# Experts mixed with tokens on the partitions, the residual carried into the banks by identity products, and the last norm taken per partition

## The chip, the cores and the metric

The kernel runs on one core of one Trainium2 chip. The metric is the device time of one execution in microseconds (us). Engines are named as the profile names them: PE is TensorE (matrix products), PEld its weight loads, DVE is VectorE, ACT is ScalarE, POOL is GpSimd, SP is SyncE, which here only issues transfers. A "bank" is one of the eight accumulators that PE writes, 128 partitions by 512 fp32 columns.

## The reference, cut to what matters

The program is a three-layer model on 256 tokens of width 1024, all in fp32. Only its end is touched. There, each of 16 experts picks its 32 tokens, the weighted expert outputs are added to the residual, and a last RMS norm over the 1024 features of each token ends the program:

```
x = x + expert_choice_ffn(rms_norm(x, norm_ffn), router, exp_gate, exp_up, exp_down)
return rms_norm(x, norm_final)

def rms_norm(x, g, eps=1e-6):
    y = x * rsqrt(mean(x * x, axis=-1) + eps)     # mean over the 1024 features of a token
    return y * g

# in expert_choice_ffn, for expert e with its 32 tokens idx[e] and their weights vals[e]
y[e]  = (silu(xg[e] @ w_gate[e]) * (xg[e] @ w_up[e])) @ w_down[e] * vals[e]
out   = zeros(256, 1024); out[idx[e]] += y[e]      # over all experts
```

## The kernel before, in words

**Layout.** The residual is held transposed, in the tile `residual_T` (`m.xT`): eight pieces of 128 features on the partitions by 256 tokens. `normed_T` (`hT`) has the same shape and holds normed activations or squares. A sum over the features of a token is then a sum over partitions, which PE makes by a product with a matrix of ones (`sum_of_squares`, L461 to L470).

**Weights.** All weights come from memory in 378 chunks of 1 MB (16 tiles of 128x128). 370 of them go through a ring of six slots, `weight_ring`, issued by SP in the loop L2217 to L2224: a slot is filled again once PE has signalled, on its next fed product, that it has used it up (`Feed.pass_on`, L397). The last eight chunks are brought early into a region of the arena by ACT (L1451).

**Experts.** For each expert x (L1100 to L1127), PE makes gate, up and down products, each from four chunks, the 32 tokens of the expert being the stationary side (`quarters`). The four quarters of the output width stand on four groups of 32 partitions. In between come two pairs of transposes (`flip`, L416), whose results ACT and DVE copy. DVE copies the expert's output to `m.ye` (L2110, signal `e_y`). Then eight products "mix" the expert into banks 4 to 7 (L1124 to L1126): the stationary side is a piece of `ye`, the moving side is `m.comb`, the 32 rows by 256 tokens that say which token takes which output with which weight. The banks hold features on the partitions and tokens along the row, and are accumulated over all 16 experts. They were cleared by products with zeros (L1098).

**The end.** After the last mix (signal `e_mix`), DVE adds each bank to the residual (L2115), DVE and ACT square the eight pieces (L2118, L1482), PE sums the squares over the partitions into bank 5 (L1132), ACT takes the root of 128x256 copies of the sums (L1485), DVE its reciprocal (L1555), DVE multiplies the eight pieces by it and by the gain (`normalise`, L1558), PE transposes all of them back to tokens on the partitions (16 flips, L1138), ACT and DVE copy the banks to the arena (L1487, L2123), and SP stores each half of 128 tokens (L2225 to L2229). Each step waits for the one before it on another engine. The engines' orders are written out by hand; nothing else plans them.

Of the kernel before, what the change touches and what calls it, by code (L numbers as in the profile page):

```python
# [9 lines left out]
ALU = mybir.AluOpType  # L10
ACT = mybir.ActivationFunctionType
# [51 lines left out]
def columns():  # L63
# [9 lines left out]
        ("q_norm", 1), ("k_norm", 1), ("norm_ffn_2", KD), ("norm_final", KD), ("rel_bias", HEADS),  # L73
# [79 lines left out]
X_FLIP = {"in": 0, "out": 4}  # L153
# [6 lines left out]
class Signals:  # L160


    def __init__(self, nc, ctx):
        def sem(name):
# [13 lines left out]
        (self.x_flip, self.xT, self.square, self.square_v, self.sumsq, self.both, self.weights, self.root, self.normed, self.h, self.res, self.first_a, self.first_v,  # L178
         self.mod_sum, self.mod_row, self.mod_cols, self.mod, self.mod_acc) = [sem(n) for n in (
            "x_flip", "xT", "square", "square_v", "sumsq", "both", "weights", "root", "normed", "h", "res", "first_a", "first_v",  # L180
# [38 lines left out]
        self.out_even, self.out_odd = [sem(n) for n in ("out_even", "out_odd")]  # L219
# [17 lines left out]
class Memory:  # L237


    def __init__(self, nc, ctx):  # L240
# [91 lines left out]

        a = Arena(area, n)
        self.htok_ = a.take(NT * D)
        self.htok = tiles(self.htok_, D)
# [68 lines left out]
def tensor_program(e, m, s, feed):  # L404
# [193 lines left out]
    e.wait_ge(s.late, 16)  # L598
# [501 lines left out]
    for x in range(EXPERTS):  # L1100
# [23 lines left out]
        for j in range(4):  # L1124
            for a in range(2):
                ins = mm(B[4 + j][:, a * T:(a + 1) * T], m.ye[32 * j:32 * j + 32, a * P:(a + 1) * P], m.comb[32 * j:32 * j + 32, :], False, False)  # L1126
        ins.then_inc(s.e_mix, 1)  # L1127

    e.wait_ge(s.xT, 8 * NORM_OUT + KD)
    for k in range(KD):  # L1132
        if k % 2:
            e.wait_ge(s.square, squares_before(NORM_OUT) + k + 1)
        else:
            e.wait_ge(s.square_v, k // 2 + 1)
        sum_of_squares(NORM_OUT, k)
    for j in range(NT):  # L1138
        for q in range(2):
            for c in range(4):  # L1140
                e.wait_ge(s.normed, 8 * NORM_OUT + 4 * q + c + 1)
                ins = flip(B[2 * j + q][:, c * P:(c + 1) * P], hT[:, 4 * q + c, j * P:(j + 1) * P])
            ins.then_inc(s.x_flip, 1)


def scalar_program(e, m, s, dram):
# [1240 lines left out]
```

## Time and profile before

| what | value |
|---|---|
| median of 3 runs | 1902.39 us (1899.36 to 1904.59) |
| the profiled execution's own time | 1904.66 us |
| its span, first to last instruction | 1902.9 us |
| PE busy | 1573.6 us, 83% of the span |
| DVE busy | 549.2 us, 29% |
| ACT busy | 259.3 us, 14% |
| read from memory | 402.69 MB |
| mean granted TensorE clock | 0.906 of full speed |

The times of the program fall into three stages: up to about 1415 us the layers before the experts, then the 16 experts up to 1882.8 us, and the end behind the last mix, 20.1 us. Which engine or transfer bounds a stage is read from the rows of that stage, not from the shares of the whole span.

### The profile page before, as it was taken

The numbers are of one execution on the slowest core, as the hardware profiler recorded it, in microseconds if no ns is written. First come the engines' busy times: TensorE is split into PE (matmuls) and PEld (weight loads), VectorE is DVE, ScalarE is ACT, GpSimd is POOL, SyncE is SP. The second block draws the span as 40 slices with busy tenths as digits, with TensorE's granted clock in tenths as the row PEclk, the third lists the DMA queues.
The fourth block names the chain that finished last, engine by engine and source line by source line (L and its number), as shares of the span: only waits on it lengthen the run. The fifth ranks groups of instructions, "written<-read, shape, count | busy, mean of one in ns | idle before, by whom it ended". The sixth has DMA issues, their size and how long they took to land.

```text
span 1902.9 us, 25312 instructions
## 1 busy us (share of the span) xinstructions
PE 1573.6 (83%) x11140; PEld 1152.3 (61%) x11140; DVE 549.2 (29%) x1199; ACT 259.3 (14%) x618; POOL 72.0 (4%) x96
## 2 busy tenths in 40 slices
PE   7979999998879999999878879998866656666666
PEld 4857788886637888878656657776732222222223
DVE  3670444301132311033647554323220000000002
ACT  2330100002212000001323222220100000000001
POOL 0120000000000000000110111200000000000000
PEclk8989999998979999999988999999988787778787
DMA  8466578744343644333100001323629999999992
GB/s 359 155 258 248 218 279 318 278 142 155 133 155 121 236 151 155 138 128 133 68 24 24 2 24 45 114 108 126 250 87 421 422 420 421 421 421 420 419 421 105
DMA packets 57485, 405.39 MB, mean 213 GB/s; under 512 B 6168, under 2 KB 8344, under 8 KB 8864
## 3 DMA queue, kind: packets, MB, share of 16 engines
q1 hardware_dynamic: 53984, 390.35, 52.5%
q10 hardware_dynamic: 3392, 13.42, 1.8%
q8 instruction: 88, 1.44, 0.3%
q14 instruction: 21, 0.17, 0.0%
HBM read 402.69 MB, written 1.06 MB: 212 GB/s over the span
## 4 chain that ended last, share of the span: by engine, by line
PE 65%; DMA 23%; DVE 9%; ACT 2%; issue 1%; POOL 0%; ACTq 0%; SPq 0%; POOLq 0%; DVEq 0%
PE bank L409 63%; DMA weight_ring<-weights 22%; DVE arena L1499 3%; PE bank L416 2%; DVE arena L1505 2%; ACT arena L1151 1%; DVE arena L1502 1%; DVE arena L1830 1%; DVE rstd L1555 1%; DVE normed_T L1505 0%; DMA arena<-x 0%; DVE rstd L1897 0%; DVE arena L1692 0%; DVE arena L1828 0%; ACT normed_T L1151 0%
## 5 line engine op out<-in xcount | busy, mean ns | idle before, releaser
L409 PE MATMUL bank<-normed_T,weight_ring 128*128 128x256 f32 x2640 | 608.1, 388 | 27.0 <-ACT arena L1151 12.4
L409 PEld LDWEIGHTS bank<-normed_T,weight_ring 128*128 128x128 f32 x2640 | 504.5, 194 | 108.1 <-ACT arena L1151 18.0
L409 PE MATMUL bank<-weight_ring,arena 128*32 128x256 f32 (+1 forms) x2976 | 270.0, 484 | 146.9 <-DMA weight_ring<-weights 138.5
L409 PE MATMUL bank<-arena,weight_ring 128*128 128x256 f32 x1456 | 329.6, 384 | 9.7 <-ACT arena L1151 6.8
L409 PEld LDWEIGHTS bank<-arena,weight_ring 128*128 128x128 f32 x1456 | 279.5, 193 | 51.0 <-issue 8.5
L409 PEld LDWEIGHTS bank<-weight_ring,arena 128*32 128x32 f32 (+1 forms) x2976 | 100.7, 132 | 302.9 <-DMA weight_ring<-weights 206.5
L1151 ACT ACTIVATE arena<-bank 128x256 f32<-128x256 f32 (+4 forms) x299 | 109.9, 374 | 1171.2 <-PE bank L409 625.1
L409 PE MATMUL bank<-arena 64*64 64x64 f32 (+7 forms) x3096 | 225.7, 283 | 28.4 <-DVE arena L1499 14.1
L409 PEld LDWEIGHTS bank<-arena 64*64 64x64 f32 (+5 forms) x3096 | 167.3, 155 | 97.5 <-issue 48.6
L1505 DVE SCALAR_TENSOR_TENSOR arena<-arena,bank 128x256 f32<-128x256 f32 x141 | 59.4, 422 | 544.1 <-PE bank L409 276.4
L416 PE MATMUL bank<-packed_consts,arena 128*128 128x128 f32 (+1 forms) x166 | 42.8, 358 | 65.1 <-DVE arena L1502 35.6
L416 PEld LDWEIGHTS bank<-packed_consts,arena 128*128 128x128 f32 (+1 forms) x166 | 22.6, 171 | 98.8 <-DVE arena L1502 46.1
L1505 DVE SCALAR_TENSOR_TENSOR residual_T<-bank,modulation,residual_T 128x256 f32<-128x256 f32 x32 | 15.5, 484 | 217.9 <-PE bank L409 217.9
L1505 DVE SCALAR_TENSOR_TENSOR arena<-weight_ring,silu_c,arena 128x1024 f32<-128x1024 f32 x49 | 62.8, 1282 | 1.0
L1151 ACT ACTIVATE normed_T<-residual_T 128x256 f32<-128x256 f32 x52 | 21.2, 415 | 291.3 <-DVE residual_T L1505 277.0
L409 PE MATMUL bank<-weight_ring,silu_c_copies 128*32 128x512 f32 (+1 forms) x256 | 39.7, 712 | 19.9 <-DMA weight_ring<-weights 19.9
L1151 ACT ACTIVATE arena<-arena 128x256 f32<-128x256 f32 (+3 forms) x93 | 42.0, 470 | 54.2 <-DVE arena L1692 32.2
L1499 DVE TENSOR_TENSOR arena<-arena 128x256 f32<-128x256 f32 (+4 forms) x98 | 41.1, 423 | 11.2 <-ACT arena L1151 8.0
L2110 DVE COPY arena<-bank 128x256 f32<-128x256 f32 x16 | 6.8, 425 | 129.1 <-PE bank L409 129.1
L1499 DVE TENSOR_TENSOR arena<-bank,packed_consts 128x256 f32<-128x256 f32 (+1 forms) x85 | 28.4, 369 | 41.8 <-PE bank L409 41.4
L2133 POOL TENSOR_TENSOR arena<-arena,packed_consts 128x512 f32<-128x512 f32 (+1 forms) x28 | 28.8, 1036 | 271.8 <-DVE arena L1499 192.0
L409 PE MATMUL bank<-normed_T,packed_consts 128*128 128x256 f32 x112 | 33.3, 403 | 5.6 <-DVE residual_T L1499 3.1
(119 smaller groups left out, 637.5 us busy)
## 6 DMA issues: line engine op xcount, KB each, us to landing
weight_ring<-weights SPq DMA_DIRECT2D x370, 1024.0 KB, 10.2
arena<-ahead ACTq DMA_DIRECT2D x8, 1024.0 KB, 18.0
packed_consts<-packed ACTq DMA_DIRECT2D x1, 2852.0 KB, 13.6
arena<-bias_by_distance ACTq DMA_DIRECT2D x2, 1024.0 KB, 7.0
arena<-x SPq DMA_DIRECT2D x1, 1024.0 KB, 5.2
out<-arena SPq DMA_DIRECT2D x2, 512.0 KB, 2.6
packed_consts<-packed SPq DMA_DIRECT2D x1, 254.5 KB, 2.8
bias_by_distance<-arena ACTq DMA_DIRECT2D x1, 16.0 KB
```

Source lines behind the costliest of these rows:

```text
L409: return e.matmul(out, lhsT, rhs, start=start, stop=stop, skip_group_check=True)
L416: return e.transpose(out, in_, ident[0:n, 0:n])
L1151: return e.activation(out, in_, f, **kw)
L1499: return e.tensor_tensor(out, a, b, op)
L1502: return e.tensor_scalar(out, a, s1, s2, op0, op1) if s2 is not None else e.tensor_scalar(out, a, s1, None, op0)
L1505: return e.scalar_tensor_tensor(out=out, in0=a, scalar=sc, in1=b, op0=op0, op1=op1)
L1555: link(e.reciprocal(m.rstd[:, :], m.rstd[:, :]))
L1830: link(e.reciprocal(tiles(inv_, P), F))
L2110: e.tensor_copy(m.ye, B[3][:, 0:QW]).then_inc(s.e_y, 1)
L2133: return e.tensor_tensor(out, a, b, op)
```

## The change: what it does

The mix is turned round: `m.comb` (128 of its token columns) is now the stationary side and `m.ye` the moving one, so banks 4 to 7 hold tokens on the partitions and features along the row. Bank 4 + j holds features 256 j to 256 j + 255, for tokens 0 to 127 in its left half and 128 to 255 in its right half.

The residual is brought into the same banks by PE: behind the mix of each of the first four experts stand four products with the identity matrix, 128x128 each, that transpose pieces of `residual_T` and add them to the bank.

The last norm then works per partition. ACT squares each half bank with an accumulator output (eight instructions, one number per token each). DVE multiplies each bank by the final gain, which now comes as a 128x1024 array, the same row on every partition; ACT's queue brings it in (512 KB, behind the gather copy k = 1) to the left half of `normed_T`. DVE adds up the 128x8 sums to 128x2, ACT takes the roots, DVE the reciprocals; then DVE scales tokens 0 to 127 and ACT tokens 128 to 255, each in one instruction of 128x1024, in place in `residual_T`, and SP stores each half from there. The eight columns of `norm_final` leave the packed constants.

```
@@ tensor_program
-                ins = mm(B[4 + j][:, a * T:(a + 1) * T], m.ye[32 * j:32 * j + 32, a * P:(a + 1) * P], m.comb[32 * j:32 * j + 32, :], False, False)
+                ins = mm(B[4 + j][:, a * T:(a + 1) * T], m.comb[32 * j:32 * j + 32, a * P:(a + 1) * P], m.ye[32 * j:32 * j + 32, :], False, False)
         ins.then_inc(s.e_mix, 1)
-    e.wait_ge(s.xT, 8 * NORM_OUT + KD)
-    for k in range(KD):
...
-        sum_of_squares(NORM_OUT, k)
-    for j in range(NT):
-        for q in range(2):
-            for c in range(4):
-                e.wait_ge(s.normed, 8 * NORM_OUT + 4 * q + c + 1)
-                ins = flip(B[2 * j + q][:, c * P:(c + 1) * P], hT[:, 4 * q + c, j * P:(j + 1) * P])
-            ins.then_inc(s.x_flip, 1)
+        if x < 4:
+            for a in range(NT):
+                for i in range(2):
+                    mm(B[4 + x][:, a * T + i * P:a * T + (i + 1) * P], m.xT[:, 2 * x + i, a * P:(a + 1) * P], ident, False, False)
@@ scalar_program
         act(m.xall[:, k * 512:(k + 1) * 512], B[k % 4][:, :], ACT.Copy).then_inc(s.x_odd, 1)
+        if k == 1:
+            e.dma_start(m.final_gain, dram["final_gain"]).then_inc(s.late, 16)
...
     e.preload_act_table(ACT.Sqrt)
-    for k in range(1, KD, 2):
-        e.wait_ge(s.xT, 8 * NORM_OUT + k + 1)
-        act(hT[:, k, :], xT[:, k, :], ACT.Square).then_inc(s.square, 2)
-    root(NORM_OUT)
-    res = m.htok
-    for j in range(NT):
-        e.wait_ge(s.x_flip, X_FLIP["out"] + 2 * j + 1)
-        act(res[:, j, 0:512], B[2 * j][:, :], ACT.Copy).then_inc(s.out_even, 1)
+    sums, roots = m.y_stat[:, 0:4 * NT], m.y_stat[:, 4 * NT:5 * NT]
+    e.wait_ge(s.e_mix, EXPERTS)
+    for j in range(4):
+        if j >= 2:
+            e.wait_ge(s.y_gain, 4 - j)
+        for a in range(NT):
+            act(m.y_sq[:, 4 * a + j, :], B[4 + j][:, a * T:(a + 1) * T], ACT.Square, accum_out=sums[:, 4 * a + j:4 * a + j + 1]).then_inc(s.square, 1)
+    e.wait_ge(s.sumsq, NORM_OUT)
+    act(roots, roots, ACT.Sqrt, scale=1.0 / D, bias=m.col("eps")).then_inc(s.root, 1)
+    e.wait_ge(s.normed, 8 * NORM_OUT + 1)
+    act(m.yg[:, D:2 * D], m.yg[:, D:2 * D], ACT.Copy, scale=roots[:, 1:2]).then_inc(s.out_row[1], 1)
@@ vector_program
+    def with_gain(j):
+        yg = m.yg.rearrange("p (m j n) -> p m j n", m=NT, j=4)[:, :, j, :]
+        return tt(yg, tiles(B[4 + j][:, :], T), m.final_gain[:, j * T:(j + 1) * T].unsqueeze(1).to_broadcast([P, NT, T]), ALU.mult)
+
+    e.wait_ge(s.late, LATE["final_gain"])
     e.wait_ge(s.e_mix, EXPERTS)
-    for j in range(4):
-        o = m.xT_[:, 2 * j * T:(2 * j + 2) * T]
-        tt(o, B[4 + j][:, :], o, ALU.add).then_inc(s.xT, 2)
-    for k in range(0, KD, 2):
-        e.wait_ge(s.xT, 8 * NORM_OUT + k + 2)
-        tt(hT[:, k, :], xT[:, k, :], xT[:, k, :], ALU.mult).then_inc(s.square_v, 1)
-    inverse_root(NORM_OUT)
-    normalise(hT, col("norm_final", 0, KD), s.normed)
-    for j in range(NT):
-        e.wait_ge(s.x_flip, X_FLIP["out"] + 2 * j + 2)
-        e.tensor_copy(m.htok[:, j, 512:1024], B[2 * j + 1][:, :]).then_inc(s.out_odd, 1)
+    with_gain(3).then_inc(s.y_gain, 1)
+    with_gain(2).then_inc(s.y_gain, 1)
+    for j in range(2):
+        e.wait_ge(s.square, squares_before(NORM_OUT) + NT * (j + 1))
+        with_gain(j).then_inc(s.y_gain, 1)
+    sums, roots = m.y_stat[:, 0:4 * NT], m.y_stat[:, 4 * NT:5 * NT]
+    e.wait_ge(s.square, squares_before(NORM_OUT) + 4 * NT)
+    e.tensor_reduce(roots, tiles(sums, 4), AX, ALU.add).then_inc(s.sumsq, 1)
+    e.wait_ge(s.root, NORM_OUT + 1)
+    e.reciprocal(roots, roots).then_inc(s.normed, 1)
+    e.wait_ge(s.normed, 8 * NORM_OUT + 1)
+    e.wait_ge(s.y_gain, 4)
+    ts(m.yg[:, 0:D], m.yg[:, 0:D], roots[:, 0:1], None, ALU.mult).then_inc(s.out_row[0], 1)
@@ sync_program
-        e.wait_ge(s.out_even, j + 1)
-        e.wait_ge(s.out_odd, j + 1)
-        e.dma_start(dram["out"][0, j * P:(j + 1) * P, :], m.htok[:, j, :]).then_inc(s.stored, 16)
+        e.wait_ge(s.out_row[j], 1)
+        e.dma_start(dram["out"][0, j * P:(j + 1) * P, :], m.yg[:, j * D:(j + 1) * D]).then_inc(s.stored, 16)
@@ Memory
+        a = Arena(self.hT_, KD * T)
+        self.final_gain, self.y_stat = a.take(D), a.take(5 * NT)
+        self.yg = self.xT_
```

Where the instructions stand now. First PE's queue around the mix of expert 0 (each row a run of like instructions; "arena x8" is the mix, `packed_consts` holds the identity). Before:

```order
L409 MATMUL bank<-weight_ring,arena 32x256 x32
L409 MATMUL bank<-arena 128x256 x8
L409 MATMUL bank<-weight_ring,arena 32x256 x32
L416 MATMUL bank<-packed_consts,arena 128x128 x2
L409 MATMUL bank<-weight_ring,arena 32x256 x32
```

After:

```order
L415 MATMUL bank<-weight_ring,arena 32x256 x32
L415 MATMUL bank<-arena 128x256 x8
L415 MATMUL bank<-packed_consts,residual_T 128x128 x4
L415 MATMUL bank<-weight_ring,arena 32x256 x32
L422 MATMUL bank<-packed_consts,arena 128x128 x2
L415 MATMUL bank<-weight_ring,arena 32x256 x32
```

Four products stand between the mix of expert 0 and the gate products of expert 1, and the same behind experts 1 to 3. Next DVE's queue behind the copy of the last expert's output (the first row of each piece). Before:

```order
L2110 COPY arena<-bank 128x256
L1499 TENSOR_TENSOR residual_T<-bank,residual_T 128x512 x4
L1499 TENSOR_TENSOR normed_T<-residual_T 128x256 x4
L1555 RECIPROCAL rstd<-rstd 128x256
L1505 SCALAR_TENSOR_TENSOR normed_T<-residual_T,packed_consts,rstd 128x256 x8
L2125 COPY arena<-bank 128x512 x2
```

After:

```order
L2109 COPY arena<-bank 128x256
L1498 TENSOR_TENSOR residual_T<-bank,normed_T 128x2x256 x4
L2126 TENSOR_REDUCE normed_T<-normed_T 128x2
L2128 RECIPROCAL normed_T<-normed_T 128x2
L1501 TENSOR_SCALAR residual_T<-residual_T,normed_T 128x1024
```

The 256-wide reciprocal, the eight 256-wide products and the two copies are gone; a reduction and a reciprocal of two columns and one product of 1024 columns stand in their place. PE's queue ends with the last mix. ACT's queue from the last expert on, before:

```order
L1151 ACTIVATE arena<-bank 128x256 x32
L1481 ACT_TABLE_LOAD
L1151 ACTIVATE normed_T<-residual_T 128x256 x4
L1151 ACTIVATE rstd<-bank,packed_consts 128x256
L1151 ACTIVATE arena<-bank 128x512 x2
```

After:

```order
L1145 ACTIVATE arena<-bank 128x256 x32
L1477 ACT_TABLE_LOAD
L1145 ACTIVATE arena,normed_T<-bank 128x256 x8
L1145 ACTIVATE normed_T<-normed_T,packed_consts 128x2
L1145 ACTIVATE residual_T<-residual_T,normed_T 128x1024
```

ACT now squares all eight pieces, straight from the banks, and scales one half of the result.

## Rows read from the trace of the kernel before

**Rows 1.** Busy time by stretch: us, then each engine's, PEclk, DMA share, GB/s.

```profile
1500.00:1860.00 360.00, 228.45 (x2520) 89.95 (x2512) 22.84 (x69) 7.90 (x24) 0.00 (x0) 0.79 1.01 421
1868.60:1882.80 14.20, 12.53 (x164) 6.09 (x164) 1.70 (x4) 1.94 (x3) 0.00 (x0) 0.83 0.00 1
1882.80:1902.90 20.10, 10.34 (x32) 7.20 (x32) 10.22 (x19) 3.33 (x7) 0.00 (x0) 0.69 0.13 52
1396.00:1415.00 19.00, 17.99 (x39) 7.40 (x37) 3.04 (x6) 2.39 (x4) 0.20 (x1) 0.92 0.00 0
```

**Rows 2.** Chain of waits behind the last mix: start us, us, what.

```profile
1881.58 1.24 PE bank L409 x16
...
1882.92 2.50 DVE residual_T L1499 x4
...
1885.84 5.39 PE bank L409 x16
...
1891.76 1.76 DVE rstd L1555
...
1894.09 4.97 PE bank L416 x16
...
1899.08 0.69 DVE arena L2125
```

**Rows 3.** Timeline of SP's issues at the end; then DMAs by kind, us to landing.

```profile
1898.16 2.03 SPq L2228 DMA_DIRECT2D out<-arena  x2
...
out<-arena SPq DMA_DIRECT2D x2, 512.0 KB, 2.6
```

**Rows 4.** Timeline of ACT in a softmax: start us, us, what.

```profile
1250.05 0.48 ACT L1151 ACTIVATE arena<-bank,arena 128x256 f32<-128x256 f32 x1 [1.29 <-DVE arena L2006]
1250.42 0.19 ACT L1151 ACTIVATION_READ_ACCUMULATOR arena<-bank,arena 128x1 f32 x1
1250.52 0.46 ACT L1151 ACTIVATE arena<-bank,packed_consts 128x256 f32<-128x256 f32 x1
```

**Rows 5.** ACT's instructions by form: busy us, mean ns, idle before.

```profile
L1151 ACT ACTIVATE arena<-bank 128x256 f32<-128x256 f32 x235 | 88.1, 383 | 1076.6 <-PE bank L409 585.1 <-PE bank L416 483.9 <-DVE arena L1499 6.9
...
L1151 ACT ACTIVATE normed_T<-residual_T 128x256 f32<-128x256 f32 x52 | 21.2, 415 | 291.3 <-DVE residual_T L1505 277.0 <-DVE residual_T L1499 11.1 <-DVE residual_T L1584 2.9
...
L1151 ACT ACTIVATE normed_T<-normed_T,modulation 128x256 f32<-128x256 f32 x32 | 13.2, 496 | 7.2 <-DVE normed_T L1505 7.2
...
L1151 ACT ACTIVATE arena<-arena 128x512 f32<-128x512 f32 x5 | 2.7, 617 | 0.0
L1151 ACT ACTIVATE arena<-arena 128x1280 f32<-128x1280 f32 x2 | 2.5, 1270 | 1.1 <-DVE arena L1502 1.1
...
L1151 ACT ACTIVATE arena<-arena,packed_consts 128x10 f32<-128x10 f32 x1 | 0.3, 302 | 0.0
```

**Rows 6.** DVE's instructions by form.

```profile
L1502 DVE TENSOR_SCALAR arena<-weight_ring,silu_c 128x1024 f32<-128x1024 f32 x7 | 5.2, 748 | 0.0
...
L2045 DVE RECIPROCAL arena<-arena 128x1 f32<-128x1 f32 x2 | 0.3, 159 | 0.1
...
L2039 DVE TENSOR_REDUCE arena<-bank 128x1 f32<-128x16 f32 x2 | 0.3, 175 | 7.0 <-PE bank L409 7.0
```

**Rows 7.** Timeline around expert 0's mix, SP and PE.

```profile
1438.45 1.17 PE L409 MATMUL bank<-arena 32*128 32x256 f32 x16 [0.55 <-DVE arena L2110]
...
1439.55 1.07 PE L409 MATMUL bank<-weight_ring,arena 128*32 128x256 f32 x16
...
1441.89 1.07 PE L409 MATMUL bank<-weight_ring,arena 128*32 128x256 f32 x16 [1.27 <-DMA weight_ring<-weights]
```

**Rows 8.** Tile weight_ring from 1440 to 1860 us: its DMAs.

```profile
DMA to landing us min/median/max: 9.2/11.6/13.2
```

**Rows 9.** The page's costliest groups: PE's products with 128x128 weights.

```profile
L409 PE MATMUL bank<-normed_T,weight_ring 128*128 128x256 f32 x2640 | 608.1, 388 | 27.0 <-ACT arena L1151 12.4
...
L409 PE MATMUL bank<-arena,weight_ring 128*128 128x256 f32 x1456 | 329.6, 384 | 9.7 <-ACT arena L1151 6.8
```

More of the change, by code:

```diff
@@ L72, in columns @@
         ("a0", 2 * KR), ("k_k", KR), ("k_a", KR), ("r_k", KR), ("ln_w", KR), ("ln_b", KR), ("pool_scale", KR),
-        ("q_norm", 1), ("k_norm", 1), ("norm_ffn_2", KD), ("norm_final", KD), ("rel_bias", HEADS),
+        ("q_norm", 1), ("k_norm", 1), ("norm_ffn_2", KD), ("rel_bias", HEADS),
         ("w2", RW), ("a2", RW), ("g2", RW), ("pool_w", 4 * P), ("router", KD * EXPERTS),
@@ L152 @@
 QK_A = {"rsqrt": 1, "v": 2}
-X_FLIP = {"in": 0, "out": 4}
+LATE = {"consts": 16, "final_gain": 32}
 FIRST_A = {"tanh_c": 1, "ln_lambda": 2}
@@ L176, in __init__ @@
         self.col, self.col_out = sem("col"), sem("col_out")
-        (self.x_flip, self.xT, self.square, self.square_v, self.sumsq, self.both, self.weights, self.root, self.normed, self.h, self.res, self.first_a, self.first_v,
+        (self.x_flip, self.xT, self.square, self.sumsq, self.both, self.weights, self.root, self.normed, self.h, self.res, self.first_a, self.first_v,
          self.mod_sum, self.mod_row, self.mod_cols, self.mod, self.mod_acc) = [sem(n) for n in (
-            "x_flip", "xT", "square", "square_v", "sumsq", "both", "weights", "root", "normed", "h", "res", "first_a", "first_v",
+            "x_flip", "xT", "square", "sumsq", "both", "weights", "root", "normed", "h", "res", "first_a", "first_v",
             "mod_sum", "mod_row", "mod_cols", "mod", "mod_acc")]
@@ L218, in __init__ @@
             "g4", "e_gate", "g_flip", "comb", "e_tanh", "e_up", "e_act", "e_hid", "e_flip", "e_hidT", "e_down", "e_y", "e_mix")]
-        self.out_even, self.out_odd = [sem(n) for n in ("out_even", "out_odd")]
+        self.y_gain, self.out_row = sem("y_gain"), [sem(f"out_row{j}") for j in range(NT)]
 class Unit:
@@ L594, in tensor_program @@
     ffn(0, NORM_FFN0, KD, NORM_KV, lambda f: steps(early, share(f, KF, 6 * PER_VECTOR)))
-    e.wait_ge(s.late, 16)
+    e.wait_ge(s.late, LATE["consts"])
     mm(B[4][0:HEADS, :], m.col("rel_bias", 0, HEADS)[0:BUCKETS + 1, :], m.col("onehot", 0, 2 * T)[0:BUCKETS + 1, :], True, True).then_inc(s.rel, 1)
@@ L1582, in vector_program @@
     for i in range(4):
-        e.wait_ge(s.x_flip, X_FLIP["in"] + i + 1)
+        e.wait_ge(s.x_flip, i + 1)
         e.tensor_copy(m.xT_[:, 2 * i * T:(2 * i + 2) * T], B[i][:, :]).then_inc(s.xT, 2)
@@ L1714, in weigh @@
             g = col("final_norm", 0, KD)
-            e.wait_ge(s.late, 16)
+            e.wait_ge(s.late, LATE["consts"])
             link(tt(m.gain_sq, g, g, ALU.mult))
@@ L2165, in pool_program @@
         e.memset(un.XF, 0.0).then_inc(s.zeroed, 1)
-    e.wait_ge(s.late, 16)
+    e.wait_ge(s.late, LATE["consts"])
     level = tiles(col("level", 0, LEVELS * HALF), HALF)
@@ L2333, in pack_columns @@
         put(n, np.tile(x[f"{n}_2"].reshape(-1, 1), (2, 1)))
-    vec("norm_ffn_2", x["norm_ffn_2"]); vec("norm_final", x["norm_final_2"])
+    vec("norm_ffn_2", x["norm_ffn_2"])
     put("rel_bias", x["rel_bias"].T)
@@ L2378 @@
     nc = bacc.Bacc("TRN2", target_bir_lowering=False, num_devices=1)
-    shapes = {"weights": (RING_CHUNKS, P, TPC * P), "ahead": (AHEAD, P, TPC * P), "packed": (P, NCOLS), "x": (T, D)}
+    shapes = {"weights": (RING_CHUNKS, P, TPC * P), "ahead": (AHEAD, P, TPC * P), "packed": (P, NCOLS), "x": (T, D), "final_gain": (P, D)}
     dram = {n: nc.dram_tensor(n, a, F32, kind="ExternalInput").ap() for n, a in shapes.items()}
@@ L2384 @@
     chunks = pack_weights(x, order)
-    arrays = {"weights": chunks[:RING_CHUNKS], "ahead": chunks[RING_CHUNKS:], "packed": pack_columns(x), "x": np.ascontiguousarray(x["x"][0])}
+    arrays = {"weights": chunks[:RING_CHUNKS], "ahead": chunks[RING_CHUNKS:], "packed": pack_columns(x), "x": np.ascontiguousarray(x["x"][0]),
+              "final_gain": np.tile(x["norm_final_2"], (P, 1))}
     return run_bass_kernel_spmd(nc, [arrays], core_ids=[0]).results[0]["out"]
```

5 lines of the change are left out of this document (1 added, 4 removed).

## The prediction

> **What bounds the kernel now.** I read the busy time by stretch first. Over 360 us of the experts the transfers are busy all the time (share 1.01, 421 GB/s) while PE works 228 us of 360: this stage is paced by the weight stream, at 1.05 MB / 421 GB/s = 2.49 us a chunk, and PE has about a third of it free [rows 1]. Behind the last chunk PE finishes the last expert alone (1868.6 to 1882.8 us, PE busy 12.5 of 14.2), and then come 20.1 us in which no engine is busy for more than about half [rows 1]. The chain of waits shows why: DVE, PE, ACT, DVE, PE, DVE hand the same data on, each waiting for the one before: 2.50 us of adding banks to the residual, the rest of the squares, 5.39 of sums on PE, the root, 1.76 of reciprocal, the first products, 4.97 of transposes, the last copy of 0.69, which ends at 1899.77 [rows 2]. From the end of the last mix as DVE sees it (1882.92) to there are 16.85 us. From 1899.77 to the end of the span at 1902.9 are 3.13 us, the second store. The first was issued at 1898.16, the two issues ended at 1900.19, and each landed 2.6 us after its issue [rows 3]. So the change works on a stretch where every microsecond is on the path, and adds work only where PE waits for weights.
>
> **The change, part by part.**
>
> *The mix turned round.* The same eight products, 32 rows deep, 128 columns of weights by 256 columns moving, only with the sides exchanged, behind the same wait for `e_y`. The mix takes 1.17 us [rows 7]. Cost 0; the last mix still ends at about 1882.82.
>
> *Identity products.* Four for each of experts 0 to 3. A fp32 product shows as two records, so eight records of 128 columns an expert. No row shows one; from below, the mix's 1.17 us for 16 records gives 0.6 us for eight, from above the sums' 5.39 us for 16 records give 2.7 us [rows 2, 7]. I take 2.5, near the 16 transposes of 128 columns, 4.97 us, halved [rows 2]. What hides it: after the mix of expert 0 PE began the next chunk at 1439.55 with no wait and ended it at 1440.6, and then waited 1.27 us for the chunk at 1441.89 [rows 7]. With 2.5 us more it begins that first chunk at 1442.05, one chunk late, and has caught up within two, since a chunk takes 1.07 us of PE and 2.49 us of the stream. Behind these products on PE's queue stands the signal that frees a ring slot, so a transfer could be issued late. But a chunk lands 11.6 us after its issue [rows 8], which is 11.6 / 2.49 = 4.7 chunks: the queue holds more than three chunks (over 7 us) behind the one that is running, and a slot freed 2.5 us late never empties it. Cost 0; without that cover 4 x 2.5 = 10 us.
>
> *The gain's transfer.* 512 KB, issued by ACT during the gather. The transfers are idle there (share 0.00 from 1396 to 1415), ACT is busy 2.4 us of 19 [rows 1]. The array is needed 480 us later. Cost 0 (at full rate it would be 1.25 us of the stream if it fell into it).
>
> *Squares.* From 1882.92, ACT, eight of 128x256 from a bank, each followed by a read of the accumulator. In the softmax the pair with a bias per partition takes 0.47 us from start to start (1250.05 to 1250.52) [rows 4]. Squares have no such operand; it costs 496 - 415 = 81 ns in the rows with and without [rows 5]. So 0.39 us a pair, 7 x 0.39 + 0.47 for the last = 3.2 us. Bounds: 8 x 0.33 = 2.6 if the reads are quite hidden (383 ns less the overlap of about 0.05), 8 x (0.383 + 0.19) = 4.6 if nothing overlaps [rows 4, 5]. A rule gives less: the Trainium skill, "ScalarE: Activation LUTs", section "What ACT_TABLE_LOAD costs", has 186 ns + 0.833 ns a column with 93 ns of overlap between neighbours, 0.31 us a square, 2.5 us in all. It has no price for the accumulator read, which these rows do show; by it the end would come 0.7 us sooner.
>
> *Gain products.* DVE, four of 128x512 with one side in a bank; the four adds of that shape take 2.50 us, 0.63 each [rows 2]. Banks 7 and 6 are done at +1.3, before ACT wants bank 6 (+1.6). Then bank 4 and bank 5 as ACT has squared them (+0.8, +1.6), done at +2.6. That is hidden under the 3.2 us of squares, with 0.6 us to spare. If the squares take only 2.6, DVE is level with them.
>
> *The statistics.* Reduction 128x2 out of 8 columns: 0.175 and a hand-over of 0.05. Root with a bias per partition: 0.30 and 0.05. Reciprocal of two columns: 0.16 and 0.05 [rows 5, 6]. Sum 0.79 us, in place of 5.39 of sums on PE and 1.76 of reciprocal, with a root between them [rows 2].
>
> *Scaling.* DVE 128x1024: 0.75 us [rows 6]. ACT 128x1024: between 617 ns for 512 and 1270 ns for 1280 columns lies 0.617 + 512 x 0.850/1000 = 1.05 us, plus 0.08 for the scale per partition and 0.05 hand-over = 1.18 [rows 5]. ACT's half ends last. It replaces the first normalised pieces, the transposes and the copies.
>
> *Sum.* 3.2 + 0.79 + 1.18 = 5.2 us from 1882.92, so the last writer ends at 1888.1 instead of 1899.77: 16.85 - 5.2 = 11.65 us less.
>
> *Stores.* In the old order the issues were about 1.7 us apart, now about 0.4, so both 512 KB transfers are under way at once. At the experts' rate each needs 0.52 MB / 421 GB/s = 1.25 us of the 16 engines [rows 1]. If the second waits for the first it lands up to 1.25 - 0.4 = 0.85 us later; 0 if the 2.6 us are mostly latency. I take 0.4. In the Trainium skill, "DMA: Bandwidth & Descriptors", section "Issuing engines are not separate DMA queues", transfers share the same 16 engines, and its "Anatomy of one DMA" gives 2.0 us + bytes / 436 GB/s, 3.2 us for one store. The trace has 2.6. By the page both stores together would take 4.4 us from the first issue, about 1 us worse than my 3.4.
>
> Net gain 11.65 - 0.4 = 11.25 us. The span goes from 1902.9 to 1891.65, the profiled execution's own time from 1904.66 to 1893.4. The median of the runs lies 2.27 us below that execution, so the median should be 1902.39 - 11.25 = **1891.1 us**. The bounds of the unknown terms: squares 0.6 better or 1.4 worse, stores 0.4 either way, small ones together 0.5: gain 9.0 to 12.7, median 1889.7 to 1893.4.
>
> **The rivals.**
>
> 1. *Nothing overlaps in the new tail*: accumulator reads serial (+1.4), stores one behind the other (+0.45), and the two-column instructions waiting as long again as they work (+0.8). Gain 8.6, 1893.8 us. Against it speaks the pair in the softmax, where the read starts 0.37 us after an activation of 0.48 us and the next starts 0.47 after it [rows 4].
>
> 2. *The identity products stall the stream*: each expert's 2.5 us goes straight into the time, because slots come free late. +10 us, net gain 1.3, 1901.1 us, no change. For it: the freeing signal does stand behind them. Against it: 11.6 us from issue to landing [rows 8], and PE's third of free time [rows 1].
>
> 3. *Slower: everything behind the constants moves.* The packed constants lose eight columns, so `residual_T`, `normed_T` and the arena start 32 bytes lower on each partition. If an address mattered to PE's moving reads, the price would fall on the 2640 + 1456 records with 128x128 weights, mostly in the layers before the experts, where PE waits little [rows 9]. It decides from 11.25 us / 4096 = 2.7 ns a record, and the kernel is slower by over 0.3% from 4.1 ns. At 5 ns, 20.5 us: 1911.6 us. Against it: products that read from `normed_T` and from many places of the arena have the same mean, 388 and 384 ns [rows 9].
>
> **How the numbers follow.** A measurement of this kernel tells about 0.3%, 5.7 us, from no change: the three runs span 5.2 us. Forecast 0.82, rival 1 0.12, rival 2 0.04, rival 3 0.02. Faster by over 0.3% takes the forecast and rival 1, since even its 8.6 us is beyond 5.7: 0.94. Within 0.3%: rival 2, 0.04. Slower 0.02. The range takes the bounds 1889.7 to 1893.8 and the scatter of a median, about 1.5 us each way: 1888.3 to 1895.3.
>
> **What would show it.** In the new trace: the eight squares start 0.39 us apart and DVE's four gain products end before the last; the two-column steps take about 0.8 us together; ACT's 1024-column product ends last, 5.2 us behind the last mix; the span ends 3.1 to 4.0 us behind it. Around experts 0 to 3 eight records of the identity products take 2 to 3 us, DMA share stays at 1.01, and the last weight chunk lands where it did, near 1868.6. The prediction is wrong if that chunk lands later, if ACT waits for a gain product, or if the stretch behind the last mix (now 20.1 us) is longer than 11.5 us.

## The result, and the profile after

| | median of the runs, us | lowest to highest | profiled execution: own time, span | granted clock |
|---|---|---|---|---|
| before | 1900.58 (5 runs) | 1899.36 to 1904.59 | 1904.66, 1902.9 | 0.906 |
| after | 1888.83 (5 runs) | 1885.65 to 1890.72 | 1885.65, 1883.9 | 0.905 |

After over before is 0.9932, with an interval of 0.9916 to 0.9948: 12.9 us less on 1900.58, between 9.9 and 16.0. The two medians differ by 11.75 us. The forecast was 11.25 us less, ending at 1891.1; the median after lies at 1888.83, inside the range given but only 0.5 us above its low end, and the ratio applied to 1900.58 gives 1887.7, which is below that end. The same kernel, run again below, gives a ratio of 0.9940, or 11.4 us less: single runs of both kernels scatter by some 5 us, and five of each leave the difference uncertain by 3 us.

The end of the program first, since there the change should work. The chain of waits behind the last mix in the kernel after (start, us, what), which answers to [rows 2]:

```profile
1873.69 1.24 PE bank L415 x16
...
1874.95 3.04 ACT arena L1145 x16
...
1878.01 0.17 DVE normed_T L2126
...
1878.20 0.30 ACT normed_T L1145
...
1878.53 0.18 DVE normed_T L2128
...
1878.73 1.15 ACT residual_T L1145
```

Five steps stand where eight stood, none of them on PE: squares, one reduction, the root, one reciprocal, the scaling. The last writer ends at 1879.88. The timeline of the same stretch shows what runs beside them (start, us, engine, line, operation, idle time before):

```profile
1874.95 0.38 ACT L1145 ACTIVATE arena<-bank 128x256 f32<-128x256 f32 x1 [8.57 <-PE bank L415]
1875.02 2.48 DVE L1498 TENSOR_TENSOR residual_T<-bank,normed_T 128x512 f32<-128x512 f32 x4 [1.39 <-PE bank L415]
1875.23 0.19 ACT L1145 ACTIVATION_READ_ACCUMULATOR arena<-bank 128x1 f32 x1
1875.32 0.38 ACT L1145 ACTIVATE arena<-bank 128x256 f32<-128x256 f32 x1
...
1878.73 0.75 DVE L1501 TENSOR_SCALAR residual_T<-residual_T,normed_T 128x1024 f32<-128x1024 f32 x1
1879.51 0.82 SPq L2233 DMA_DIRECT2D out<-residual_T  x2
```

The squares start 0.35 to 0.37 us apart. DVE's four gain products end at 1877.50, before the last square's accumulator is read (1877.98): they are hidden. The two stores are issued 0.4 us apart, from 1879.51. How long they took to land, min, median and max:

```profile
DMA to landing us min/median/max: 2.6/3.1/3.6
```

Before, both took 2.6 [rows 3]. One still does, the other takes 1.0 us more. Busy time by stretch in the kernel after (columns as in [rows 1]):

```profile
6.00:76.00 70.00, 63.37 (x303) 48.14 (x304) 31.94 (x60) 16.94 (x38) 1.56 (x3) 0.93 0.72 283
1500.00:1860.00 360.00, 232.12 (x2536) 91.13 (x2536) 23.51 (x72) 7.97 (x24) 0.00 (x0) 0.79 1.01 418
1862.42:1874.93 12.51, 10.78 (x164) 5.69 (x164) 1.69 (x4) 1.94 (x3) 0.00 (x0) 0.96 0.01 1
1874.93:1883.90 8.97, 0.00 (x0) 0.00 (x0) 3.56 (x7) 4.47 (x18) 0.00 (x0) 0.62 0.29 117
```

And the first stretch in the kernel before:

```profile
6.00:76.00 70.00, 61.95 (x293) 47.00 (x294) 30.68 (x59) 15.19 (x34) 0.13 (x1) 0.90 0.71 283
```

The stretch behind the last mix is 8.97 us instead of 20.08. But the two spans differ by 19.0, not 11.1. I cut every trace at the same three events: GpSimd's memset at the start of the experts, the landing of the last weight chunk, and the end of the last mix.

| us | start of experts | stream | last expert | tail | span |
|---|---|---|---|---|---|
| before | 1411.17 | 457.39 | 14.26 | 20.08 | 1902.9 |
| after | 1405.03 | 457.39 | 12.51 | 8.97 | 1883.9 |
| difference | 6.14 | 0.00 | 1.75 | 11.11 | 19.0 |

The stream did not move at all. The last expert ran the same 164 PE records at a granted clock of 0.96 instead of 0.83 [rows 1], and so took 1.75 us less. The 6.14 us lie ahead of the experts, and there the change touches only addresses, 4 KB of constants and, 11 us before the experts, the gain's transfer. A third of them is there when GpSimd starts its first product, at 74.48 us instead of 76.61; over the first 76 us the granted clock was 0.93 against 0.90. The rest does not show in the clock, whose mean up to the experts is 0.95 in both, and PE's work there is only 1.6 us shorter (1255.30 for 1256.86 us busy): most of the 6.14 us is time in which PE stood idle. So one profiled pair is not evidence for more than the 11.1 us; the experiments ask whether the other 7.9 belong to the change or to the execution.

### The profile page after: what moved, and what is told of

It is laid out like the page before. It is cut to its first block, busy times and chain, and to the rows that moved or that the text cites. A ratio compares the mean times of both kernels' runs of the same rounds, so it can differ in the third digit from the quotient of the medians.

```text
span 1883.9 us, 25306 instructions
## 1 busy us (share of the span) xinstructions
PE 1568.1 (83%) x11140; PEld 1147.1 (61%) x11140; DVE 542.3 (29%) x1187; ACT 260.3 (14%) x629; POOL 72.0 (4%) x96
## 4 chain that ended last, share of the span: by engine, by line
PE 65%; DMA 23%; DVE 9%; ACT 2%; issue 1%; POOL 0%; ACTq 0%; SPq 0%; POOLq 0%; DVEq 0%
PE bank L415 63%; DMA weight_ring<-weights 22%; DVE arena L1498 3%; PE bank L422 2%; DVE arena L1504 2%; ACT arena L1145 1%; DVE arena L1501 1%; DVE arena L1829 1%; DVE rstd L1554 0%; DVE normed_T L1504 0%; DVE rstd L1896 0%; DMA arena<-x 0%; DVE arena L1691 0%; DVE arena L1827 0%; ACT normed_T L1145 0%
## 5 line engine op out<-in xcount | busy, mean ns | idle before, releaser
L415 PE MATMUL bank<-weight_ring,arena 128*32 128x256 f32 (+1 forms) x2976 | 274.4, 491 | 138.8 <-DMA weight_ring<-weights 129.9
L1504 DVE SCALAR_TENSOR_TENSOR arena<-arena 128x128 f32<-128x128 f32 (+3 forms) x96 | 36.5, 430 | 2.4 <-POOL arena L2139 2.0
```

The source lines that it names most:

```text
L415: return e.matmul(out, lhsT, rhs, start=start, stop=stop, skip_group_check=True)
L1504: return e.scalar_tensor_tensor(out=out, in0=a, scalar=sc, in1=b, op0=op0, op1=op1)
```

## The experiments

Twelve more runs were made, two of them of the two kernels unedited. Each is compared with runs of the kernel before on the same chip. The table has, for each, the four parts of its profiled execution and its median.

| us | start of experts | stream | last expert | tail | median (runs) | ratio and interval |
|---|---|---|---|---|---|---|
| a_again | 1406.06 | 457.57 | 12.58 | 8.89 | 1889.72 (6) | 0.9940, 0.9922 to 0.9959 |
| before_again | 1408.78 | 457.17 | 12.03 | 20.02 | 1899.70 (10) | 0.9994, 0.9983 to 1.0005 |
| pad8 | 1410.38 | 457.37 | 14.28 | 8.97 | 1890.42 (6) | 0.9944, 0.9923 to 0.9965 |
| no_ident | 1410.37 | 457.40 | 14.26 | 8.97 | 1888.41 (6) | 0.9942, 0.9923 to 0.9960 |
| ident_x4 | 1409.89 | 458.76 | 12.02 | 8.93 | 1890.78 (9) | 0.9946, 0.9931 to 0.9960 |
| ident_x8 | 1408.86 | 467.02 | 12.04 | 8.88 | 1902.27 (12) | 1.0007, 0.9994 to 1.0020 |
| ident_last | 1410.81 | 457.29 | 12.03 | 9.97 | 1891.91 (1) | |
| ident_alone | 1408.56 | 457.38 | 14.26 | 15.90 | 1896.45 (10) | 0.9976, 0.9967 to 0.9985 |
| rows_in_banks | 1410.18 | 457.88 | 13.23 | 8.61 | 1891.66 (1) | |
| pipelined | 1406.21 | 457.81 | 13.22 | 7.96 | 1890.40 (6) | 0.9953, 0.9936 to 0.9971 |
| split_store | 1407.80 | 457.34 | 12.03 | 8.73 | 1890.22 (5) | 0.9943, 0.9929 to 0.9956 |

The shared medians of before are 1901.42, 1901.85, 1901.15 and 1901.18 us. The twelfth, one_store, is read by its tail alone.

### The two kernels again: a_again, before_again

Both unedited.

> The changed kernel once more, unedited. Its tail behind the last mix took 8.97 us where the kernel before took 20.08, so the theory that the tail is the whole gain expects 11.1 us between the medians and a tail of 8.97 us again, whatever the time before the experts does. The theory that the change also speeds up the layers before the experts (the address shift) expects 15 to 19 us, as between the two first profiled executions (1902.9 and 1883.9 us of span).

> The kernel before, unedited, for its three stretches in another execution. If the stages before the experts differ between executions and not between kernels, the experts' start falls anywhere between 1404 and 1412 us here as in the changed kernel, the weight stream takes 457.4 us from there, the last expert 12.5 or 14.3, and the stretch behind the last mix 20.08 us again. If the address shift had sped up the first layers, the start stays at 1411 us or later.

The tail repeats: 8.89 after 8.97, and 20.02 after 20.08. The start of the experts does not: 1406.06 and 1405.03 for the kernel after, 1408.78 and 1411.17 for the kernel before. The difference between the kernels' medians is 11.7 us here (1901.42 less 1889.72). before_again measures the ruler: the same kernel against itself, 1.7 us below its neighbours' median of 1901.42, ratio 0.9994.

### The addresses: pad8

```diff
-        ("q_norm", 1), ("k_norm", 1), ("norm_ffn_2", KD), ("rel_bias", HEADS),
+        ("q_norm", 1), ("k_norm", 1), ("norm_ffn_2", KD), ("unused", KD), ("rel_bias", HEADS),
```

> The changed kernel with eight unused columns left where the last norm's gain stood in the packed constants, so that every tile behind them has its old address. If the address shift of 32 bytes matters, this run is 2 to 8 us slower than the unedited changed kernel of the same call; if only the tail matters, it is the same within 2 us and its tail is again 8.97 us.

With all addresses back where they were, the experts start at 1410.38 us. With the new addresses (no_ident, below) they start at 1410.37. So the 6.14 us of the first pair are not the price of the addresses: the nine profiles at the new addresses (one_store apart) spread from 1405.03 to 1410.81, the four at the old ones (before, before_again, ident_alone, pad8) from 1408.56 to 1411.17. Median 1890.42 against 1889.72 is inside both spreads. What this does not exclude is a difference of about 1 us in favour of the new addresses: the means of these starts are 1408.4 and 1409.7, and only the new ones ever start before 1408. Rival 3, which had them 20 us slower, is refuted all the same.

### Are the identity products hidden? no_ident, ident_x4, ident_x8, ident_last

no_ident leaves the residual out of the banks, so it computes the norm of the mix alone:

```diff
-        if x < 4:
-            for a in range(NT):
-                for i in range(2):
-                    mm(B[4 + x][...], m.xT[:, 2 * x + i, a * P:(a + 1) * P], ident, False, False)
```

> Leaves out the identity products, so the residual is missing from the result. If they are hidden behind the weight stream (eight records take 1.16 us behind expert 0, and PE then waits less), time and the length of the stream from the first freed slot to the last chunk's landing are the same within 1 us. If they stall the stream, this is 4 x 1.2 = 5 us faster.

Stream 457.40 us without the products, 457.39 with them; tail 8.97 and 8.97. In the kernel after they look like this on PE, behind the mix of expert 0, which answers to [rows 7]:

```profile
1432.45 1.17 PE L415 MATMUL bank<-arena 32*128 32x256 f32 x16 [0.55 <-DVE arena L2109]
1433.55 1.16 PE L415 MATMUL bank<-packed_consts,residual_T 128*128 128x128 f32 x8
1434.64 1.07 PE L415 MATMUL bank<-weight_ring,arena 128*32 128x256 f32 x16
1435.92 1.07 PE L415 MATMUL bank<-weight_ring,arena 128*32 128x256 f32 x16 [0.21 <-DMA weight_ring<-weights]
```

Eight records cost 1.16 us, not the 2.5 I took; PE's next wait for a chunk is 0.21 us instead of 1.27 [rows 7]. The price is less than that idle time, so not even the next chunk is late.

The execution of one_store (below), in which PE's granted clock had a mean of 0.664 instead of 0.905, tests the cover in a harder case. There the same eight records took nearly the 2.5 us of the prediction:

```profile
1887.50 2.08 PE L415 MATMUL bank<-packed_consts,residual_T 128*128 128x128 f32 x8
```

and the transfers around them went on at their full share (columns as in [rows 1]):

```profile
1880.00:1910.00 30.00, 22.76 (x220) 9.93 (x220) 1.96 (x6) 0.66 (x2) 0.00 (x0) 0.62 1.01 420
```

Its whole stream took 458.38 us.

ident_x4 and ident_x8 add, to each of the four products, three and seven that add zero:

```diff
                     mm(B[4 + x][...], m.xT[:, 2 * x + i, a * P:(a + 1) * P], ident, False, False)
+                    for _ in range(3):        # ident_x8: range(7)
+                        mm(B[4 + x][...], m.zeros, ident, False, False)
```

> 16 products instead of four behind the mixes of experts 0 to 3 (12 with zeros as weights). With 32 products the group took 7.3 us at the higher clock and the stream took 467.0 us instead of 457.4 from the start of the experts to the landing of the last chunk. With 16 it takes 3.7 us (5 at the lower clock). The theory of the cover (a freed slot may come late by what is queued behind the running transfer, 7 us or more, less the 1.9 us of the mix and its wait) expects 457.4 us again and no change in time against the changed kernel; a theory of proportion (9.6 us for 28 more products) expects 461.5.

> 32 products instead of four behind the mix of each of experts 0 to 3 (28 of them with zeros as weights, so the result stays). That is 8 x 1.16 = 9.3 us of PE an expert at the higher clock, up to 18 at the lower. PE has about 11.5 us free of 29.8 an expert, and the queue holds 7 us of transfers. The theory of the cover (slack in PE plus queued transfers) expects little at the higher clock, 0 to 4 us in all, and up to 4 x 7 = 28 us at the lower; a theory in which every microsecond behind the mix is on the path expects 4 x 8.1 = 32 us or more at either.

ident_x8 shows where the cover ends: it lost more than the 0 to 4 us that I expected at the higher clock. Behind expert 0 its 64 records take 7.3 us (1437.26 to 1444.60), and SP, which waits for the slot signals, issues nothing for 10.1 us (1435.19 to 1445.25). Behind the next three experts SP is silent for 10.1, 11.7 and 12.3 us; behind the last two the mix and a part of the products ran at the lower clock. The stream is 9.6 us longer. Three windows of it (columns as before):

```profile
1440.00:1470.00 30.00, 23.10 (x274) 13.99 (x274) 1.96 (x6) 0.66 (x2) 0.00 (x0) 0.89 0.96 396
1500.00:1530.00 30.00, 21.75 (x247) 14.15 (x244) 1.27 (x3) 0.66 (x2) 0.00 (x0) 0.90 0.90 374
1530.00:1560.00 30.00, 23.33 (x244) 14.94 (x248) 1.96 (x6) 0.74 (x2) 0.00 (x0) 0.78 0.87 356
```

The loss grows with the silence: the share is 0.96 around the first group and 0.90 and 0.87 around the last two, where it is 1.01 in the kernel before. The shortest time from issue to landing is

```profile
DMA to landing us min/median/max: 4.8/11.4/13.2
```

where it was 9.2 [rows 8]: a transfer that lands so soon has found few others ahead of it. ident_x4, with 4.3 us of products behind expert 0, lost 1.4 us in all, where I had expected none. There SP was silent for 8.4 us behind expert 0 (1436.67 to 1445.07) and for 6.5 us behind each of the others; the shortest landing is 6.5 us, and the share is 0.99 from 1440 to 1470 and 1.01 in the three stretches of 30 us behind it. So a silence of 6.5 us cost nothing and one of 8.4 us about 1.4. An estimate from ident_x8: its four silences add up to 44.0 us, less the 9.6 lost, which leaves 8.6 us for each that the queue bears; ident_x4 alone gives 8.4 - 1.4 = 7.0. The limit lies at 7 to 9 us. The kernel after stays silent for 3.8 us (1431.48 to 1435.29) behind expert 0 and for 4.7 at most behind the next three; in one_store it was 6.5 us behind expert 0, at a full share. Rival 2 is a real mechanism, but it needs some 2 us more of silence than the change brings. The medians go further apart than the profiles: ident_x8 lies 12.6 us above a_again, not 9.6. Its profiled execution was one of its fastest (1898.65 against a median of 1902.27); the others have no trace.

ident_last puts the same products behind the mixes of the last four experts instead of the first four:

```diff
-        ins.then_inc(s.e_mix, 1)
-        if x < 4:
+        if x >= 12:
             for a in range(NT):
                 for i in range(2):
-                    mm(B[4 + x][...], m.xT[:, 2 * x + i, ...], ident, False, False)
+                    ins = mm(B[x - 8][...], m.xT[:, 2 * (x - 12) + i, ...], ident, False, False)
+        ins.then_inc(s.e_mix, 1)
```

> The identity products stand behind the mixes of experts 12 to 15 instead of 0 to 3. The theory of the cover expects those behind 12 to 14 to stay free and those behind 15 to cost their own length, since nothing is left to wait for there: the stretch from the landing of the last weight chunk to the end of PE's work grows by 1.1 us (1.7 at the lower clock) over its 12.5 or 14.3 us, and the stretch from there to the end stays 8.95 us. If they cost nothing anywhere, it stays 12.5 or 14.3.

The last group runs from 1879.99 to 1881.15 (1.16 us), with nothing to cover it, and the tail, counted from the end of the mix, is 9.97 instead of 8.9: 1.0 to 1.1 us for one group. So the place among the first experts is worth that much, and the price itself, 1.16, is confirmed on the path.

### Which part brings the gain? ident_alone

On the kernel before: the residual is put into the banks by identity products, but the features stay on the partitions. ACT squares the eight pieces from the banks, PE sums them over the partitions, and the normalised pieces are transposed as before.

```diff
         ins.then_inc(s.e_mix, 1)
+        if x < 4:
+            for i in range(2):
+                mm(B[4 + x][:, i * T:(i + 1) * T], ident, m.xT[:, 2 * x + i, :], False, False)
...
-        o = m.xT_[:, 2 * j * T:(2 * j + 2) * T]
-        tt(o, B[4 + j][:, :], o, ALU.add).then_inc(s.xT, 2)
```

> The kernel before with one part of the change alone: the residual is brought into banks 4 to 7 by identity products (two of 256 columns behind each of the first four mixes), but the banks keep features on the partitions, so the sums over partitions on PE, the 256-column root and reciprocal and the 16 transposes all stay. Squares and the normalising products read the banks. If the gain were the removed adds, this part brings most of the 11 us. My theory is that the turned layout brings most: here the first square starts 0.6 us sooner and PE's sums 2.5 us sooner, so the stretch behind the last mix falls from 20.08 to 17.5 us, and the rest of the 11.1 us needs tokens on the partitions.

Its chain behind the last mix:

```profile
1880.66 3.73 PE bank L409 x16
...
1884.99 1.76 DVE rstd L1556
...
1887.71 4.55 PE bank L416 x15
```

The tail is 15.90 us where I expected 17.5. Of the 4.2 us that it is shorter than before, 2.5 are the adds. Most of the rest is PE's sums, 3.73 us instead of 5.39 [rows 2]. They are the same 16 records; here and in the kernel before their windows read

```profile
1880.66:1884.40 3.74, 3.72 (x16) 2.96 (x16) 0.00 (x0) 1.88 (x7) 0.00 (x0) 1.00 0.00 0
```

```profile
1885.84:1891.23 5.39, 5.38 (x16) 4.11 (x16) 0.90 (x3) 0.07 (x1) 0.00 (x0) 0.68 0.00 0
```

at a granted clock of 1.00 against 0.68. Before, PE had stood idle for 3.08 us while DVE added and squared; here it stood for 0.53 us. So the add had also cost PE part of its clock in the next step. Of the whole 11.1 us, 4.2 come with the identity products alone and 6.9 need the turned layout. The part includes that ACT squares all eight pieces straight from the banks. The whole time agrees: the ratio of 0.9976 is 4.6 us, with an interval of 2.9 to 6.3.

### Where do the stores lose? one_store, split_store

one_store leaves out the store of the first 128 tokens, so half of the output is not written:

```diff
-    for j in range(NT):
-        e.wait_ge(s.out_row[j], 1)
-        e.dma_start(dram["out"][0, j * P:(j + 1) * P, :], m.yg[:, j * D:(j + 1) * D]).then_inc(s.stored, 16)
+    e.wait_ge(s.out_row[0], 1)
+    e.wait_ge(s.out_row[1], 1)
+    e.dma_start(dram["out"][0, P:2 * P, :], m.yg[:, D:2 * D]).then_inc(s.stored, 16)
```

> Leaves out the store of tokens 0 to 127. In the changed kernel the last writer ends 4.0 us before the end of the span, in the kernel before 3.13. If the 0.9 us are the two transfers sharing the engines, the single store brings it back to 3.1 and its landing to 2.6 us after issue (3.6 for the second store now). If they come from where the data lies or from the order of issue, it stays at 3.9 to 4.0.

This one execution had a granted clock of 0.664 and a span of 2338.3 us; the tail holds no PE work, so it can be read. Why its clock was low is not known. The steps of ACT are the same as in the kernel after, and the store, by the page's list of DMA issues, lands in 2.6:

```profile
2330.29 3.04 ACT arena L1145 x16
...
2334.08 1.15 ACT residual_T L1145
```

```profile
out<-residual_T SPq DMA_DIRECT2D x1, 512.0 KB, 2.6
```

From the end of the last writer (2335.23) to the end of the span are 3.07 us; in the kernel after they are 4.02. The data lies where it did and is issued as late as before; only the other transfer is gone. So the 0.95 us are the price of having two under way at once, as far as one execution can show it.

split_store sends the first row block in two halves and gives DVE 192 of ACT's 1024 columns:

```diff
-    act(m.yg[:, D:2 * D], m.yg[:, D:2 * D], ACT.Copy, scale=roots[:, 1:2])
+    act(m.yg[:, D:D + 832], m.yg[:, D:D + 832], ACT.Copy, scale=roots[:, 1:2])
...
-    ts(m.yg[:, 0:D], m.yg[:, 0:D], roots[:, 0:1], None, ALU.mult)
+    for h in range(2):
+        ts(m.yg[:, h * 512:(h + 1) * 512], m.yg[:, h * 512:(h + 1) * 512], roots[:, 0:1], None, ALU.mult)
+    ts(m.yg[:, D + 832:2 * D], m.yg[:, D + 832:2 * D], roots[:, 1:2], None, ALU.mult)
```

> The changed kernel with its layout and its mix as they are; only the last step is cut finer. DVE scales tokens 0 to 127 in two halves of 512 columns, each stored at once (256 KB), and then 192 columns of the second half, of which ACT scales 832. The first store is issued about 0.35 us sooner and the last writer ends about 0.15 us sooner. If the end is held by the transfer engines from the first store on, the stretch behind the last mix falls from 8.95 to 8.6 us, with the mix still at 1.17 us (in the two kernels with rows in banks the mix took 2.36 us and ate what they gained). If it is held by the last store's own way, it falls by 0.15 only. Three transfers in place of two may also cost: then 8.9 or more. Median: as the changed kernel, within 2 us.

The tail is 8.73 us, 0.2 less than the 8.9 of its neighbours. The last writer is now DVE:

```profile
1880.97 0.49 DVE residual_T L1501
1881.46 0.40 DVEq L2243
1881.86 0.23 DVE residual_T L1501
```

It ends at 1882.09, but SP begins the last store only at 1882.36, because it is still issuing the second of the small ones until 1882.31; and the last store lands 3.1 us after its issue, not 2.6. The finer cut won 0.5 us on one side and gave back 0.3 on SP. A gain of 0.2 us can't be told in the whole time (1890.22), so this is not a better version that I could claim.

### Another layout: rows_in_banks, pipelined

rows_in_banks lets each bank hold one block of tokens, so that ACT needs four squares of 512 columns instead of eight of 256. Two quarters of the mix, from different 32-row strips of the array, then write one bank, and the kernel orders them by a wait in the middle:

```diff
-        for j in range(4):
+        for j in (0, 2, 1, 3):
+            if j == 1:
+                ins.then_inc(s.x_flip, 1)
+                e.wait_ge(s.x_flip, 4 + x + 1)
             for a in range(2):
-                ins = mm(B[4 + j][:, a * T:(a + 1) * T], ...)
+                ins = mm(B[4 + 2 * a + j // 2][:, (j % 2) * T:(j % 2 + 1) * T], ...)
```

> Banks 4 and 5 hold tokens 0 to 127, banks 6 and 7 tokens 128 to 255, so ACT squares four pieces of 512 columns instead of eight of 256, and DVE's gain products need no stepped pattern. Two quarters of the mix now write one bank, so the mix is split in two halves with a wait between them. An ACT instruction has a fixed part: eight squares took 3.03 us; four of 512 columns should take 4 x 0.60 = 2.4. DVE's four gain products (2.48 us) are then level. The wait in the mix adds 0.1 to 0.2 us, in the last expert on the path. Stretch behind the last mix 8.95 -> 8.3 us. If the squares went by columns alone, it stays at 8.9.

The squares became cheaper (2.66 us with a wait in between, for 3.03), but ACT now waits for a gain product, and the mix pays 1.2 us where I expected 0.1 to 0.2:

```profile
1881.34 1.30 DVE residual_T L1500 x2
```

```profile
1878.86 2.36 PE L415 MATMUL bank<-arena 32*128 32x256 f32 x16 [0.55 <-DVE arena L2111]
```

The tail is 8.61 us, 0.3 to 0.4 less, and the mix 2.36 instead of 1.17: a net loss of 0.9 us (last expert and tail 21.84, against 12.03 + 8.9 = 20.9).

pipelined adds to that: statistics of the first 128 tokens while ACT squares the second, the first block scaled and stored in two pieces, the second shared by ACT (640 columns) and DVE (384).

> The same layout, and each half of the tokens gets its statistics as soon as its two banks are squared; the first half is stored in two pieces of 256 KB, and ACT and DVE share the scaling of the second half (640 and 384 columns). The one-store run showed that the end is held by the two stores sharing the transfer engines. If so, starting to store about 1 us sooner brings the stretch behind the last mix from 8.95 to 7.6 to 8.0 us. If the last store's own way (3.1 us from the last writer) holds it, 8.0 to 8.3. The time of the whole cannot show it: 1 us is 0.05%, and medians of six differ by 1 to 2 us; expected median 1888 to 1890.

Its tail is 7.96 us, the shortest of all. With the 1.2 us that the mix costs more, it stands 0.2 us behind the kernel after; the median of 1890.40 can't tell them apart. Whether a layout can have the short tail without the ordered mix was not tried.

## Where the prediction was right, and what failed in it

- **The mix turned round, cost 0.** Held: 1.17 us, and the stream unchanged.
- **Identity products, 2.5 us each and hidden.** Hidden, yes (457.39 against 457.40 without them). The size was wrong: 1.16 us. I went by half of the 16 transposes [rows 2] without reading the clock beside them. Their window in the kernel before is

```profile
1894.09:1899.06 4.97, 4.95 (x16) 3.05 (x16) 3.41 (x8) 1.19 (x2) 0.00 (x0) 0.50 0.01 6
```

a granted clock of 0.50, behind 2.87 us of idle. And the first seven of them started 0.40 us apart, as DVE delivered the normalised pieces (eight in 3.26 us), so the row held waits besides. That 4.97 / 4 = 1.24 us, an estimate for half of them at the full clock, comes close to the 1.16 is thus partly chance. At a low clock 2.5 was nearly right: 2.08 us in one_store. The cover, "over 7 us", came out at 7 to 9 us by ident_x4 and ident_x8.
- **The gain's transfer, cost 0.** Held; it is issued at 1394.02 and lands in 3.6 us, in the idle stretch of the transfers.
- **Squares, 3.2 us.** 3.03 (1874.95 to 1877.98), the pairs 0.36 apart instead of 0.39. The rule of the Trainium skill ("ScalarE: Activation LUTs", "What ACT_TABLE_LOAD costs") had 0.31; with the accumulator read that it has no price for, the pair costs 0.05 more than that.
- **Gain products done at +2.6.** 1877.50, +2.57, hidden.
- **Statistics 0.79, scaling 1.18.** 0.75 (1877.98 to 1878.73) and 1.15.
- **Last writer 5.2 us behind the squares' start.** 4.93.
- **Stores, +0.4 us, bounds 0 to 0.85.** This term was mis-sized: 4.02 instead of 3.13 behind the last writer, +0.9, just past the upper bound, and in one_store the whole of it goes with the other transfer. I had taken the middle between "latency" and "one behind the other"; it is the latter. The second store landed 3.6 us after its issue where the sum had 3.0, so from the first issue to the last landing are 4.0 us where I had 3.4; the span ends 0.4 us behind that. The Trainium skill ("DMA: Bandwidth & Descriptors", "Anatomy of one DMA", a section on transfers that GpSimd issues) gave 3.2 us for one store and 4.4 for both. The trace, with stores issued by SP, agrees with neither: 2.6 for one in one_store and 4.0 for both.
- **The tail as a whole.** Forecast 11.25 us shorter, measured 11.11. The error of +0.49 in the stores and the −0.35 of the steps ahead of them nearly cancel; that the total came within 0.14 us is luck.
- **The rivals.** Rival 1: one of its three parts came true (the stores one behind the other), the other two did not. Rival 2 is refuted by no_ident, and its threshold is bracketed by ident_x4 and ident_x8. Rival 3 is refuted by pad8.
- **The step that failed: the level, "the scatter of a median, about 1.5 us each way".** The forecast subtracted 11.25 us, right to 0.14 in the tail, from 1902.39, the median of three runs. Every later median of that kernel is lower: 1900.58, 1901.42, 1901.85, 1901.15, 1901.18, and 1899.70 for before_again. From 1901.2, the middle of these six, the same sum gives 1889.9. And the scatter comes in twice, once with the base and once with the result: the medians of the kernel after and of its two equals, pad8 and no_ident, are 1888.83, 1889.72, 1890.42 and 1888.41. Each set spans 2.0 to 2.2 us. So the range should have reached some 3 us below the forecast for the scatter of both medians alone, before any term of the change; it reached 2.8 with everything. The mechanism of the tail and of the cover held. Single runs span 1893.3 to 1904.9 us for before.

What stays open: the four medians after have a mean of 1889.3, 11.9 us below 1901.2, and the parts of the profiles that the change touches add up to 11.1. The surplus of 0.8 us is within what the medians scatter; it could also be a small effect of the new addresses, which the starts of the experts above leave room for. Telling the two apart would take more profiles at either address. What makes one execution reach the experts 6 us sooner than another is open too.

## What to carry to other kernels

At the end of this program a norm along the partitions cost a chain that crosses engines at every step (sums on PE, transposes, copies); if the last products can be turned so that the norm's axis lies along the free dimension, the sums come with the squares, the transposes and copies go, and what must be added can be summed in the banks earlier, where PE waits for weights anyway. To judge such a cover, count not PE's idle share but the longest silence of the signal that frees a buffer against what is queued. And before explaining a difference between two profiles, cut both at the same events: here 7.9 of 19.0 us belonged to the two executions and not to the change.

## What the runs showed of the hardware beyond the forecast

- **The clock follows short idle times.** PE's 16 sums took 3.73 us at a granted clock of 1.00 after 0.53 us of idle, and 5.39 at 0.68 after 3.08. A weight chunk takes 1.07 us at a granted clock of 1.00 (2.4 GHz) and 1.93 at 0.50 (1.2 GHz).
- **The same 457 us, whatever PE does.** The stage paced by transfers took between 457.17 and 457.88 us in eleven profiles, with the identity products and without, while the stage ahead of it, in which PE is busy 89% of the time, spread from 1405.03 to 1411.17, 0.4%. Most of the scatter between profiles comes from there, up to 2.3 us more from the last expert (12.02 to 14.28 us). In one_store, at a granted clock of 0.664, the stage ahead took 1856.2 us and the stream 458.38: a third more time in one, 0.2% in the other.
- **Two stores of 512 KB, issued 0.4 us apart**, landed in 2.6 and 3.6 us; one alone in 2.6. Two of 256 KB landed in 2.2 each, with a third of 512 KB behind them at 3.1.
- **Two strips of PE's rows writing one bank in order** doubled the mix, 1.17 to 2.36 us: the trace has eight records from 1878.86 (1.17 us) and eight from 1880.08 (1.17 us), where the kernel after has all sixteen in 1.17. With the wait between them the two halves run one behind the other.
